# A hybrid encoder block: gate items moved between key-value items, mLSTM decays made ahead of their scores

## The reference

```
xn     = rmsnorm(x)
proj   = xn @ w_in     # stick-breaking q,k,v | mLSTM q,k,v,i,f,o | memory q | 3 x 1024 gate columns
A      = stick-breaking attention, 8 heads x 64, strictly causal
B      = mLSTM, 4 heads x 128, chunkwise with a running maximum; rmsnorm; * sigmoid(o)
C      = cross attention into 256 memory tokens, 4 heads x 128, keys and values = rmsnorm(mem) @ w_mem_kv
merged = sum over the 3 branches of sigmoid(gate + b_gate) * (branch @ its own 512 x 1024 matrix)
h      = x + merged @ w_out
out    = h + PEER(rmsnorm(h))    # 16384 one-neuron experts, 8 product-key heads, the 16 best of each
```

## Time and profile before

| | us |
|---|---|
| runs | 1713.17, 1718.76, 1719.29; median 1718.76 |
| profiled execution | 1713.92 |
| its span, first to last instruction | 1712.2 |
| busy: PE, DVE, ACT, POOL | 1664.0, 1083.4, 758.2, 424.9 |
| mean granted TensorE clock | 0.993 |

### The profile page before, as it was taken

The page is one execution under the profiler, slowest core; times in us unless marked ns, Lnnn a source line. Parts: engine busy times, 40 slices in busy tenths (PEclk is TensorE's granted clock), DMA queues, the critical chain, the costliest instruction groups (busy, mean ns, idle before and its releaser), DMA issues.

```text
span 1712.2 us, 23937 instructions
## 1 busy us (share of the span) xinstructions
PE 1664.0 (97%) x8260; PEld 1359.2 (79%) x8260; DVE 1083.4 (63%) x1869; ACT 758.2 (44%) x931; POOL 424.9 (25%) x188
## 2 busy tenths in 40 slices
PE   7999989999999899999999999999999999999998
PEld 6888767777777688888878888888788888888886
DVE  3017442334677278999988888853466666666664
ACT  5232254632543433444545555554444444444442
POOL 4444543223244333688850000000000000000000
PEclk9999999999999999999999999999999999999999
DMA  5222233321163322366557788876898888988883
GB/s 188 96 98 99 100 109 99 102 77 63 68 227 141 111 74 98 126 219 220 207 201 270 289 304 295 290 296 219 284 344 287 290 288 284 294 287 290 283 292 123
DMA packets 164265, 343.84 MB, mean 201 GB/s; under 512 B 11496, under 2 KB 77032, under 8 KB 162024
## 3 DMA queue, kind: packets, MB, share of 16 engines
q1 hardware_dynamic: 164200, 342.98, 57.8%
HBM read 267.43 MB, written 75.50 MB: 200 GB/s over the span
## 4 chain that ended last, share of the span: by engine, by line
PE 66%; DVE 13%; issue 12%; POOL 5%; ACT 2%; DMA 2%; DVEq 0%; POOLq 0%; SPq 0%; ACTq 0%
PE ps L903 27%; PE ps L894 14%; PE ps L569 11%; POOL w_r L381 5%; PE ps L931 3%; PE ps L816 3%; PE ps L582 3%; DMA uraw<-in_u 1%; DVE picks L1656 1%; PE ps L680 1%; DVE picks L1646 1%; DVE cand L1623 1%; DVE top_small L1659 1%; PE ps L728 1%; DVE top_small L1609 1%
## 5 line engine op out<-in xcount | busy, mean ns | idle before, releaser
L903 PE MATMUL ps<-v_r,w_pairs 128*128 128x512 f32 x2048 | 466.2, 390 | 3.2 <-DVE w_pairs L1742 3.2
L903 PEld LDWEIGHTS ps<-v_r,w_pairs 128*128 128x128 f32 x2048 | 385.6, 188 | 83.7 <-DVE v_r L1739 3.6
L894 PE MATMUL ps<-hT_r,u_r 128*128 128x512 f32 x1024 | 405.8, 396 | 1.8 <-ACT act_stage L1222 1.2
L894 PE MATMUL ps<-x_two,u_r 128*128 128x512 f32 x1024 | 399.0, 390 | 0.0
L381 POOL TENSOR_TENSOR w_r<-w_raw,w_r 128x1024 fp32r<-128x1024 f32 x102 | 256.3, 2514 | 375.0 <-ACT w_r L1017 375.0
L1739 DVE TENSOR_TENSOR v_r<-vraw,v_r 128x1024 fp32r<-128x1024 f32 x128 | 156.9, 1226 | 144.1 <-ACT v_r L1270 144.1
L1270 ACT ACTIVATE v_r<-vraw 128x1024 fp32r<-128x1024 f32 x128 | 135.7, 1060 | 251.6 <-PE ps L903 248.4
L569 PE MATMUL ps<-xT_r,w_r 128*128 128x512 f32 x1008 | 236.7, 393 | 4.5 <-DVE pre_stage L1414 3.5
L894 PEld LDWEIGHTS ps<-hT_r,u_r 128*128 128x128 f32 x1024 | 192.3, 188 | 41.7 <-issue 1.6
L569 PEld LDWEIGHTS ps<-xT_r,w_r 128*128 128x128 f32 x1008 | 188.0, 189 | 44.4 <-DVE pre_stage L1414 4.1
L894 PEld LDWEIGHTS ps<-x_two,u_r 128*128 128x128 f32 x1024 | 192.5, 188 | 37.8
(11 more groups left out here) (237 smaller groups left out, 1718.6 us busy)
## 6 DMA issues: line engine op xcount, KB each, us to landing
uraw<-in_u SPq DMA_DIRECT2D x128, 512.0 KB, 3.8
vraw<-in_v SPq DMA_DIRECT2D x128, 512.0 KB, 5.2
w_raw<-in_w SPq DMA_DIRECT2D x102, 512.0 KB, 3.5
acts_out<-act_stage SPq DMA_DIRECT2D x128, 256.0 KB, 2.2
gates<-stage SPq DMA_DIRECT2D x16, 2048.0 KB, 7.4
g_in<-gates SPq DMA_DIRECT2D x32, 1024.0 KB, 8.3
act_in<-acts_out SPq DMA_DIRECT2D x128, 256.0 KB, 5.2
gates_pre<-pre_stage SPq DMA_DIRECT2D x24, 256.0 KB, 2.4
```

Source lines behind the costliest of these rows:

```text
L894: ins = pe.matmul(bank(s % 2), u2[s][:, w, k * P:(k + 1) * P], x2[:, k, :] if w else hr4[:, 0, k, :], start=i == 0, stop=i == 15, skip_gro ...
L903: ins = pe.matmul(bank(2 * q + h), w2[:, s, w, q * P:(q + 1) * P], v2[s][:, w, h * BANK:(h + 1) * BANK], start=start and w == 0, stop=stop ...
```

## The change

It has seven parts.

- Gate items 0 to 3 move into the key-value items: two key-value items, one gate item, four times. `KV_AT` and `gate_at` give the new places, `weights_of` the weights that SP loads for a place. The value sums move to banks 2 and 3.
- Each head pair has three gate items in place of four; the two suffix sums stand behind each other. The mLSTM part has four (17 to 20), and 21, 22 and 23 lie around the memory attention, the last one between its third head's turns and product.
- `r_max` is written to DRAM (4 rows of 2 KB) and read back into all partitions as `r_all` (8 KB in each, 1 MB). The matmul with `sel3` goes, and `sel` with it.
- The four heads have a buffer each (`ew`). The decays are computed and exponentiated, and the mask put on, before the scores: heads 0 and 1 at the end of the last head pair, 2 and 3 behind its values. After the scores only `weigh` is left.
- The heads go two by two: both scores, a gate item, both values, a gate item.
- The turns of the mLSTM output move ahead of the last memory head's product. The first branch writes `mergedT` itself, so it isn't cleared; the branch banks start at 0, and the output product waits for 20 and 24 `br_used` (its two halves).
- `TURN_AFTER` goes from (20, 31, 42, 49) to (20, 32, 43, 49).

```diff
+KV_AT = (34, 35, 37, 38, 40, 41, 43, 44)
+GATES_IN_KV = 4
+def gate_at(m):
+    return I_KV + 2 + 3 * m if m < GATES_IN_KV else I_G + m
+def weights_of(n):
+    if n in KV_AT:
+        return I_KV + KV_AT.index(n)
+    return I_G + (n - I_KV - 2) // 3 if I_KV <= n < I_G + GATES_IN_KV else n
-EXP_AFTER, TURN_AFTER = (10, 20, 31, 42), (20, 31, 42, 49)
+EXP_AFTER, TURN_AFTER = (10, 20, 31, 42), (20, 32, 43, 49)
+        ew = lk + aw
...
# POOL
-            low_ws(0, I_G + 19)
+            low_ws(0, I_G + 18)
             for h in range(MLH):
-                pool.wait_ge(w_ready, h + 1)
-                keep_causal(lk[h % 2], w_masked)
-                if h >= 1:
-                    low_ws(I_G + 18 + h, 1)
-            low_ws(I_G + 22, 4)
-            pool.wait_ge(mlT_done, MLH)
-            pool.memset(mergedT, 0.0).then_inc(m_zero, 1)
-            low_ws(I_BR + 2, ITEMS - I_BR - 2)
+                pool.wait_ge(e_ready, h + 1)
+                keep_causal(ew[h], e_masked)
+            low_ws(I_G + 18, ITEMS - I_G - 18)
# SP
+            sp.wait_ge(rows_made, 1)
+            sp.dma_start(acts_dram[0, 0:4, :], r_max).then_inc(max_out, 16)
+            loaded = I_KV + 2
             for m in range(24):
-                load_item(I_G + m + 4, (I_G + m) % 4)
+                while loaded <= gate_at(m) + 4:
+                    load_item(loaded, loaded % 4)
+                    loaded += 1
+                if m == 1:
+                    sp.wait_ge(max_out, 16)
+                    sp.dma_start(r_all, acts_dram[0, 0:4, :].rearrange("h t -> (h t)").partition_broadcast(P)
+                                 ).then_inc(max_in, 16)
                 sp.wait_ge(pre_out, m + 1)
# PE
             for b in range(2):
+                if b == 1:
+                    pe.wait_ge(n_out, 4 * TT)
                 for j in range(4):
-                    n = I_KV + 4 * b + j
-                    n_item(n, n % 2, j, 4 + MT * b, mr4, MT)
+                    n = KV_AT[4 * b + j]
+                    n_item(n, n % 2, j, (4, 2)[b], mr4, MT)
+                    if j % 2:
+                        gate_item(2 * b + j // 2)
...
             for p in range(PAIRS):
+                m = GATES_IN_KV + 3 * p
                 sb_scores(p)
-                gate_item(4 * p)
+                gate_item(m)
                 if p >= 1:
                     sb_values(p - 1)
-                gate_item(4 * p + 1)
+                gate_item(m + 1)
                 sb_suffix(2 * p)
-                gate_item(4 * p + 2)
                 sb_suffix(2 * p + 1)
-                gate_item(4 * p + 3)
+                gate_item(m + 2)
...
-                pe.matmul(bank(6), sel3[:, h, :], r_max, start=True, stop=True)
...
+            for h in (0, 2):
+                ml_scores(h)
+                ml_scores(h + 1)
+                gate_item(17 + h)
                 ml_values(h)
-                if h + 2 < MLH:
-                    ml_scores(h + 2)
+                ml_values(h + 1)
                 gate_item(18 + h)
...
                 if h + 2 < NH:
                     mem_scores(h + 2)
+                elif h == 2:
+                    gate_item(23)
+                else:
+                    turn_ml()
...
-            pe.wait_ge(br_used, 24)
             for b in range(2):
+                pe.wait_ge(br_used, 20 + 4 * b)
# ACT, in each pair
                 hi_part(2 * p)
-                high_ws(I_G + 4 * p + 2)
+                high_ws(n)
                 hi_part(2 * p + 1)
-                high_ws(I_G + 4 * p + 3)
+                high_ws(n + 1)
                 exp_part(2 * p)
-                high_ws(I_G + 4 * p + 4)
                 exp_part(2 * p + 1)
-                high_ws(I_G + 4 * p + 5)
+                high_ws(n + 2)
# DVE
+            def decay(h):
+                if h == 0:
+                    dve.wait_ge(max_in, 16)
+                    dve.wait_ge(cols_out, 1)
+                dve.wait_ge(*((suffix_done, SBH - 1 + h) if h < 2 else (y_done, PAIRS)))
+                for kt in range(TT):
+                    ins = dve.tensor_scalar(ew[h][:, CAUSAL_AT[kt]:CAUSAL_AT[kt] + T - kt * P],
+                                            r_all3[:, h, kt * P:T],
+                                            key_cols[:, kt * 4 + h:kt * 4 + h + 1], 0.0, ALU.subtract, ALU.max)
...
+                dve.wait_ge(e_masked, h + 1)
                 dve.wait_ge(s_ready, h + 1)
-                dve.scalar_tensor_tensor(out=lk[h % 2], in0=region(h % 2), scalar=HD_SCALE, in1=lk[h % 2],
+                dve.scalar_tensor_tensor(out=ew[h], in0=region(h % 2), scalar=HD_SCALE, in1=ew[h],
...
-                    dve.tensor_tensor(g_, bank((4 + g) % 8), g_, ALU.mult).then_inc(br_used, 1)
+                    dve.tensor_tensor(mergedT3[:, g, :] if b == 0 else g_, bank(g), g_, ALU.mult).then_inc(br_used, 1)
+                if b == 0:
+                    return
```

More of the change, by code:

```diff
@@ L775, in _, with turn_ml @@
             mem_scores(1)
-            gate_item(23)
+            gate_item(22)
+            def turn_ml():
+                pe.wait_ge(ml_normed, 1)
+                pe.wait_ge(mexp_ready, NH)
+                for h in range(MLH):
+                    for t in range(TT):
+                        ins = turn(bank(h)[:, t * P:(t + 1) * P], y_ml4[:, t, h, :])
+                    ins.then_inc(mlT_done, 1)
             for h in range(NH):
@@ L792, in _ @@
                 ins.then_inc(my_done, 1)
-            pe.wait_ge(ml_normed, 1)
-            pe.wait_ge(mexp_ready, NH)
-            for h in range(MLH):
-                for t in range(TT):
-                    ins = turn(bank(h)[:, t * P:(t + 1) * P], y_ml4[:, t, h, :])
-                ins.then_inc(mlT_done, 1)
             def branch(b):
@@ L1052, in _ @@
                         act.activation(projT3[:, 8 + g, :], conv_out[:, g % 2, :], ACT.Silu).then_inc(silu_done, 1)
-            for n in range(I_KV + 2, I_G + 2):
+            for n in range(I_KV + 2, gate_at(2) + 4):
                 high_w(n, n % 4)
@@ L1378, in _ @@
                               ALU.add).then_inc(qk_squared, 1)
+            take_gate(1)
+            take_gate(2)
             take_kv(2)
@@ L1424, in _ @@
                 low_part(2 * p + 1)
-                take_gate(4 * p + 1)
+                take_gate(m + 1)
                 if p == PAIRS - 1:
@@ L1462, in divide @@
                 ins.then_inc(num_out, 1)
-            decay(0)
-            decay(1)
-            weigh(0)
-            weigh(1)
-            take_gate(17)
-            for h in range(MLH):
+            for h in (0, 2):
+                weigh(h)
+                weigh(h + 1)
+                take_gate(17 + h)
                 divide(h)
-                if h + 2 < MLH:
-                    decay(h + 2)
-                    weigh(h + 2)
-                take_gate(18 + h)
+                divide(h + 1)
+                if h == 0:
+                    take_gate(18)
             dve.wait_ge(num_out, MLH)
@@ L1478, in _ @@
                               ALU.add).then_inc(ml_squared, 1)
+            take_gate(20)
             dve.wait_ge(ml_rooted, 1)
@@ L1513, in _ @@
                     mem_max(h + 2)
+                elif h == 2:
+                    take_gate(23)
                 dve.wait_ge(my_done, h + 1)
@@ L1543, in merged_lo @@
                                   merged_r[:, q * D:(q + 1) * D].bitcast(F32), ALU.subtract).then_inc(m_lo, 1)
-            with dve.Fori(0, 2) as b:
+            for b in range(2):
                 for i in range(4):
```

124 lines of the change are left out of this document (56 added, 68 removed).

## The result

| us | before | changed |
|---|---|---|
| median of the runs (4 each, one chip) | 1719.03 | 1687.67 |
| lowest and highest | 1713.17, 1720.45 | 1686.46, 1690.42 |
| profiled execution, span | 1713.92, 1712.2 | 1687.29, 1685.6 |
| mean granted TensorE clock | 0.993 | 0.997 |

The ratio is 0.9826, with an interval of 0.98 to 0.9852: faster, by 1.7%. The profiled execution is 26.6 us shorter; the sum said 27.1, and the forecast was 1689. The medians lie 31.4 apart, more than the sum. The executions of one kernel differ by up to some 7 us, and the longer ones have the lower mean clock: of seven of the kernel before on another chip the shortest took 1712.22 at 0.994, the longest 1719.13 at 0.988.

What follows compares the result with a forecast made beforehand. TensorE was taken as the bound, gains being its waits, four row matmuls and clock. Terms summed to 27.1 us: 1686.8 from the profiled execution, 1691.7 from the median; forecast 1689, own range 1683 to 1697, wider 1680 to 1702.

Steps and rivals of the forecast that it cites:

- Key-value items: Key-value stretch with four gate items: period 12.0, total 49.6 against 49.7 before, gain 0; interleaving worth nothing.
- First pair: First head pair: the 2.65 wait for `pre_stage` goes, the second suffix waits 0.7 for its low part; gain 2.0.
- mLSTM: mLSTM part: 39.9 us if PE never waits, against 55.1 before without one gate item; gain 15.2.
- the 4.4 of clock: mLSTM part: 4.4 us of the 15.2 gain, from scores run at the lower clock after PE had waited 2.0.
- Rival 1: mLSTM: waits (5.6) and clock loss (4.4) return, only row matmuls are saved; gain 17.1, time 1699; chance 0.15.
- the long working with T and its slacks: mLSTM: engine schedule counted from T, the end of gate 15, claiming 2 us or more slack everywhere.
- Queries and keys, memory attention, branches: Mix stage's later parts: waits hidden by moved gate items and earlier turns, plus clock at the branches; gains 0.9, 2.8, 4.1.
- Lists: Top-16 list turns behind the mix stage: moved one up item later, PE's waits go; gain 2.1, bounds 0 and 2.1.
- Rival 2: Key-value stretch: POOL's low parts are stretched beside DVE, costing 4.7; time 1694; chance 0.12.
- Rival 3: Key-value stretch and branches: regular POOL waits keep the clock low, adding 43.5 us; time 1732; chance 0.03.
- Rival 4: PEER: the earlier start is waited away by its own transfers; time 1714 to 1719; chance 0.03.
- the 3.94 of the prediction: Key-value stretch: POOL's first part took 3.94, not 2.39, beside DVE's squares of the queries.

Runs made afterwards that it cites:

- e5: Kernel before with only the `r_max` rows written and broadcast by DMA, four-row matmuls removed; median 1705.24 of 4, ratio 0.993.
- e6: Changed kernel with an unread four-row matmul, no wait in front, ahead of each mLSTM head's scores; 1694.82 in one execution.
- e9: Kernel before with `r_max` rows by DMA, plus an unread four-row matmul ahead of each mLSTM head's scores; 1714.08 in one execution.
- e10: Kernel before with `r_max` rows by DMA, plus an unread 128-row matmul ahead of each mLSTM head's scores; 1710.87 in one execution.
- e7: Changed kernel with VectorE making six key-value-stretch low parts, query squares later, third branch item's high part before the first sigmoid; median 1681.8 of 5, ratio 0.9799.

## Why the prediction was right, and where not

**Key-value items: mis-sized by 1.1.** The mechanism held: pairs of short items stay pairs, one wait of 0.9 in each period. I had halved 5.87 after taking off a tail (2.72) and took 5.44 for a gate item. Start to start, a short item without a wait is 2.91 and a gate item 5.56, so that a period is 12.30 and not 12.0. Four of them make the 1.2 missing. The row of two items holds only one change from item to item; a period must be built from starts on both sides.

**First pair: right.** 27.30, with the waits of 0.84 for bank 7 and 0.63 (0.7 predicted) for the low part. A middle pair is 27.45 (27.4 predicted).

**mLSTM: the size right (15.6 for 15.2), two reasons wrong.** The first: I put the 4.4 of clock down to the wait. In e5, e6, e9 and e10 the clock fell in this part only where the wait and a four-row matmul came together; taking away either left it at 1.00. Rival 1 kept the waits without the row matmuls and priced the clock's 4.4 with them. e5 has such waits at 1.00, so its 10.0 was likely too much by the 4.4. The second: the long working with T and its slacks was of a thing that isn't needed, as the late decays give the same 39.49. By the runs, the rows by DMA gave 11.55, and the order two by two, by subtraction, 4.1.

**Queries and keys, memory attention, branches: 1.2, 3.8 and 4.4 for 0.9, 2.8 and 4.1.** The first two are larger than the waits that I added up. The memory part is full now, so the tails in front of its waits went as well; whether they make the whole 1.0 no run shows. At the branches the wait went from 2.37 to 1.11, 1.3 where I had 1.0; the clock is at 1.00 and gave its 1.4, and the output product's wait gave its 1.7. These make the 4.4.

**Lists: 2.1 predicted, and no run shows a gain.** The step that failed is "PE is the late one there and takes its 2.1 along". DVE's wait at the last turn did stay at 3.1, so that sign held, and yet the gain isn't there, because PE has other suppliers in this stage. Its waits for the lists and for the low parts of the up items are 2.1 + 0.5 = 2.6 before and 0.6 + 1.4 + 0.2 = 2.2 after, the last 0.2 for low parts that DVE makes. The changed kernel run again has no wait for the lists and 2.0 for POOL. The 0.6 in the table has another source. Behind the wait of 3.16 for `w_pairs` the last 64 matmuls took 16.38 in the kernel before, with a fall of the clock, and 14.79 in the changed one, without. Up to that wait the changed kernel is even 1.0 longer (1151.3 for 1150.3 from the start of the output product), of which 0.4 is the wait for `act_stage` (1.6 for 1.2). This part varies as much by itself: 1150.3 to 1152.0 in the kernel before, e5 and e9.

**The total.** That 26.6 stands beside 27.1 owes something to luck: -1.1 and -1.5 are offset by +0.4, +0.3, +1.0 and +0.3. And the forecast of 1689 lay between the value from the profiled execution (1686.8) and that from the median (1691.7); the median came out at 1687.67. What I had not priced is that the change also takes away places where the clock falls in some executions. The wait of 2.65 for `pre_stage` in the first pair is one: in the trace of before the gate item behind it ran at 1.00, but in e5, e9 and e10, which have the same wait, it fell, and the gate item took 8.48, 7.37 and 7.37 in place of 5.73. That fits medians 31.4 apart; how much of the 4.8 beyond the profiled executions is due to it no run shows.

**Rival 2** didn't come: behind the first period each low part in the stretch takes 2.4. DVE's squares of the keys were stretched in its place, as they already were in the trace of before (3.35 from 217.30 on, beside a low part of 2.40 from 217.17 on), which I had not read:

```profile
223.66 2.40 POOL L399 TENSOR_TENSOR w_r<-w_raw,w_r 128x1024 fp32r<-128x1024 f32 x1 [1.55 <-ACT w_r L1035]
```

```profile
223.78 3.36 DVE L1405 TENSOR_TENSOR qk_squares<-mem_k 128x1024 f32<-128x1024 f32 x1
```

What started first kept its length. **Rival 3** is refuted by the 1.00 of 201.69 to 252.51 with five waits for POOL of 0.88 and 1.32: the regular waits of this stretch did not keep the clock at the lower level. **Rival 4** (given back in PEER) didn't come for what the mix stage gained: PEER starts that much earlier and takes 1170.4 for 1171.0.

## What to carry to other kernels

Before crediting a reordering with a wait, ask which single part removes it: here one DMA in place of a thin matmul gave 11.55 of the mLSTM's 15.6, the pairing of heads the rest by subtraction, and the decays made ahead nothing. A wait that goes at a consumer with several suppliers is worth only what the next supplier has in hand. Price a period from start to start on both sides of an item, not from half a group, and compare stages of two versions between the same two matmuls. A stage in which the clock fell in one of two executions tells nothing of the change until that is taken out.

## What the hardware showed that I had not expected

**Behind a wait the clock falls in some executions and not in others**, at the same place. These are the places from the key-value items on at which PE waits 1.7 to 3.2 us; "four rows" and "128 rows" say what matmuls come first behind the wait, and a fall is a granted clock at or near 0.5 there:

| wait of PE | first matmuls behind it | falls |
|---|---|---|
| 1.82 to 2.02, mLSTM (before, e9) | four rows | 4 of 5 |
| 1.82, mLSTM (e5, e10) | 128 rows | 0 of 4 |
| 1.7, memory values and output product (before, e5, e9, e10) | 128 rows | 0 of 8 |
| 1.88, PEER (e10) | 128 rows | 1 of 1 |
| 2.65 and 2.66, first pair (before, e5, e9, e10) | 128 rows | 3 of 4 |
| 2.33 to 2.37, branches (before, e5, e9, e10) | 128 rows | 4 of 4 |
| 3.16, `w_pairs` (all twelve traces) | 128 rows | 5 of 12 |

The fall behind 2.37 in the kernel before:

```profile
483.17:489.00 5.83, 5.83 (x19) 4.62 (x19) 5.67 (x6) 0.34 (x1) 2.73 (x1) 0.71 0.24 89
```

A granted clock of 0.5 is 1.2 GHz; the 0.55 to 0.74 of e9 are stretches partly at it. A fall cost some 1.3 to 3.3 us where the same group of matmuls stands in another trace at 1.00. The thin matmul makes a difference at the short waits of the mLSTM, where e9 and e10 are the same but for it; the length of the wait alone doesn't decide, and what does stays open.

**VectorE and GpSimd take turns.** Five pairs of a DVE instruction with two SBUF inputs and a low part of POOL that overlap, four in the changed kernel and one in the best version (e7), show it. The one that starts first takes its normal time (2.28 for 2048 elements and 1.22 for 1024 on DVE, 2.39 on POOL), the other is longer by nearly the overlap:

| second to start | overlap with the first | longer by |
|---|---|---|
| DVE squares 204.41, POOL till 205.46 | 1.05 | 0.93 |
| POOL low part about 205.9, DVE till 207.62 | 1.7 | 1.55 |
| DVE squares of keys 223.78, POOL till 226.06 | 2.28 | 2.14 |
| DVE scaling 248.59, POOL till 250.65 | 2.06 | 1.92 |
| POOL 232.68 (best version), DVE till 233.25 | 0.57 | 0.45 |

The Trainium skill, SBUF — State Buffer, section SBUF: two separate sides, says of such pairs that they share ports under an exclusive lock, held for the whole instruction, and that the later one blocks. The trace agrees. With that page beside the 3.94 of the prediction, rival 2 would have been priced by asking who starts first at each place.

**Two prices.** The low part of an item is 1.23 on DVE against 2.40 on POOL; the profile of before had that of DVE already, in the up items whose low parts it makes (L1710, 1223 ns each). New is the decay of one head (four instructions), 1.27 from SBUF against 1.93 from PSUM.
